# Large expert units: the 32 left-over tokens' down products in fp32 on four column strips, and two down tiles in a row

## The chip, the cores and the metric

The kernel runs on one core of one Trainium2 chip. The metric is device time in microseconds of one execution of the whole program. The trace that is read here was taken by the hardware profiler in one execution of the same kernel.

## The reference

The program is a two-layer encoder on 512 tokens of width 1024: a hybrid mixer with a dense SwiGLU, then an S5 mixer with a mixture of experts. The change is in the mixture of experts alone: 8 experts, 2 per token, inner width 3584, everything float32.

```python
def swiglu(h, w_gu, w_down):
    g, u = jnp.split(h @ w_gu, 2, axis=-1)
    return (jax.nn.silu(g) * u) @ w_down
# for each block of rows (tokens routed to expert e):  swiglu(xb, w_gu[e], w_down[e])
# out[token] += gate weight * row, over the two experts of the token
```

w_gu[e] is 1024 x 7168, w_down[e] is 3584 x 1024: 44 MB of weights per expert, which must come from HBM once for each expert.

## The kernel before

**Units.** The experts are worked one after the other as eight units, four large (i = 0, 2, 4, 6) and four small ones (i = 1, 3, 5, 7), in turn. A large unit holds CAP = 160 rows: 128 and REST = 32 left-over ones; a small unit holds 128. Rows beyond that go to extra units at the end, which the profiled run's data decide.

**Weights.** A unit's weights are PER = 42 tiles of 128 x 2048 words (1 MB). SP loads them in the order in which TensorE uses them, into a ring of RING = 6 slots (expert_tiles, L1006 to L1014). A tile's load waits until the tile six places before it is split (s_ws).

**Split.** Products run in fp32r, a form in which one product of 512 columns is one pass. To keep the accuracy of fp32, each operand is split in a high part (rounded to fp32r) and a low part (the rest). ScalarE writes the high part of a tile (split, L2545), VectorE then the low part (L3553), into WSLOTS = 3 slots. Tile n + 3 may be split once TensorE is done with tile n (s_mt). A product A x B is then three products: high x high, low x high, high x low.

**A large unit** has STEPS = 14 steps of 256 inner columns (large_pe, L1949 to L1995). Step s has a gate tile and an up tile: 32 products of 320 columns (L1984: high weights against the high and low rows) and 32 of 160 (L1986: low weights against the high rows) over banks 0 to 3. ScalarE takes the low sum out of PSUM (L2580), VectorE adds the rest to it (L3586, which counts s_gs up), ScalarE makes the Silu (L2583), VectorE the product with up (L3589, s_hid). ScalarE writes its high part (L2585), VectorE the low part (L3595, L3596; s_hdr). Each of gate and up has two halves (fb = 0, 1); before TensorE starts a gate half it waits on s_gs of the step before, since it writes over the same banks.

The tiles stand in the order gate 0, up 0, gate 1, up 1, down 0, gate 2, up 2, down 1, and so on: step s's down tile is worked behind gate and up of step s + 1. A down tile has 20 products of 512 columns in `products` (L1924), for each of 2 row blocks and 2 column halves: three for the 128 rows (banks 4, 5), and two for the left-over rows (banks 6, 7). The stationary operand of the last two is a block of 128 columns: hd[:, k, P:2P] holds the left-over rows' high part in 32 columns and their low part in the next 32, the rest is zero; hz holds the high part in 32 columns and zeros. At the end of the unit ScalarE copies the low part's products out of PSUM (L2594) and VectorE adds them to the high ones (L3605).

Between the last two down tiles TensorE transposes the rows of the next unit (turn_rows, L1932, L1936). ScalarE and VectorE bring them in high and low parts to SBUF (L2555, L3563), and the next unit's first product waits for that (rows_ready).

**A small unit** has 7 steps of 512 columns and 12 products per tile, all of them in L1924 too, and transposes of its hidden rows (L2004).

**Orders.** All engines' lists are written out by hand. In large_act and large_dve ScalarE and VectorE do, in step s: split the tile three behind the gate, the hidden rows of step s, split the tile three behind the up tile, and the one three behind the down tile. VectorE makes the low part of the hidden rows behind its split of the up tile's successor. POOL gathers the rows of the next unit (L1202, L1205) and stores the results (L1213, L1216).

**Elsewhere in the program** there is one place that already uses strips of the array: kernel_steps (L1407 to L1424) makes fp32 products with 16 stationary columns whose results go to partitions 0, 32, 64 and 96 of bank 6:

```python
        def kernel_bank(k, g, first, n):
            strip = 32 * (STEP * (k % 2) + g)
            return psum[strip:strip + GC, 6, first:first + n]
```

L1325 is a plain fp32 product of 512 columns, L1401 an fp32 transpose, L1880 the router: 4 x 8 calls of pe.matmul in fp32 with 8 stationary columns.

## Time and profile before

| what | value |
|---|---|
| median of 3 runs | 2574.84 us (2573.52 to 2577.11) |
| span of the profiled execution | 2573.5 us; the profile gives no other time of that execution |
| TensorE busy | 2442.7 us, 95% |
| VectorE, ScalarE, GpSimd busy | 65%, 50%, 8% |
| mean granted TensorE clock | 0.976 |
| HBM read, written | 496.0 MB, 45.8 MB |

The expert units run from about 1267 to 2485 us of the span. PE is TensorE, DVE VectorE, ACT ScalarE, POOL GpSimd, SPq the queue of SP. A record is one instruction as the hardware counted it; in a row, "x20" means twenty such records put together, and the duration then runs from the start of the first to the end of the last. "[0.78 <-DVE ...]" is idle time ahead of a record and what ended it.

### The profile page before, as it was taken

What the parts mean: (1) busy time and instruction counts of PE and PEld (TensorE: products, weight loads), DVE (VectorE), ACT (ScalarE), POOL (GpSimd) and SP (SyncE); (2) the same over time, 40 slices, a digit from 0 to 9 for tenths busy, and PEclk for the clock granted to TensorE, in tenths of its full rate; (3) what the DMA queues carried; (4) which work ended last, traced back from release to release, by engine and by line L of the source; (5) the groups of instructions that cost most, each with busy time, mean ns of one, the idle gap of its engine ahead of it and who ended that gap; (6) DMA issues with size and microseconds to landing.
All of it is one profiled execution on the core that took longest, in us unless ns stands there. A gap on an engine that the chain in (4) does not pass through costs nothing.

```text
span 2573.5 us, 31863 instructions
## 1 busy us (share of the span) xinstructions
PE 2442.7 (95%) x12694; PEld 1975.9 (77%) x12694; DVE 1666.8 (65%) x2031; ACT 1290.7 (50%) x1508; POOL 205.5 (8%) x204
## 2 busy tenths in 40 slices
PE   7999999999999998699699999999999999999987
PEld 4555555688888876688599888998899988998856
DVE  7996875322223343972676788668876688667865
ACT  3644351222222233662355676557765577556753
POOL 4007632000000000000100000000000000000010
PEclk9999998999999998799799999999999999999998
DMA  7669210532323224450677899778987799777961
GB/s 201 200 193 249 89 33 29 176 98 98 98 99 106 94 78 144 163 189 17 207 248 248 295 373 329 251 247 323 370 285 247 247 371 369 260 249 260 376 247 44
DMA packets 316819, 527.73 MB, mean 205 GB/s; under 512 B 19334, under 2 KB 175594, under 8 KB 314010
## 3 DMA queue, kind: packets, MB, share of 16 engines
q1 hardware_dynamic: 287594, 481.30, 54.1%
q0 software_dynamic: 5888, 25.78, 3.2%
q10 hardware_dynamic: 23184, 18.55, 2.2%
q8 instruction: 103, 1.69, 0.3%
q14 instruction: 50, 0.41, 0.0%
HBM read 496.03 MB, written 45.81 MB: 211 GB/s over the span
## 4 chain that ended last, share of the span: by engine, by line
PE 82%; DVE 10%; ACT 2%; issue 2%; POOL 2%; DMA 1%; POOLq 0%; ACTq 0%; DVEq 0%
PE psum L1924 28%; PE psum L1450 17%; PE psum L1984 12%; PE psum L1749 6%; PE psum L1986 5%; PE psum L1325 3%; PE psum L1299 2%; PE psum L2084 2%; PE psum L1522 1%; DVE stages L869 1%; DVE stages L879 1%; POOL stages L1115 1%; DVE stages L874 1%; DVE stages L870 1%; POOL stages L1118 1%
## 5 line engine op out<-in xcount | busy, mean ns | idle before, releaser
L3553 DVE TENSOR_TENSOR stages_r<-kept,stages_r 128x2048 fp32r<-128x2048 f32 x336 | 769.3, 2291 | 238.6 <-ACT stages_r L2545 237.7
L2545 ACT ACTIVATE stages_r<-kept 128x2048 fp32r<-128x2048 f32 x336 | 637.4, 1912 | 217.8 <-PE psum L1924 104.3
L1924 PE MATMUL psum<-stages_r 128*128 128x512 f32 x3136 | 738.9, 394 | 3.2 <-issue 3.2
L1924 PEld LDWEIGHTS psum<-stages_r 128*128 128x128 f32 x3136 | 584.2, 189 | 126.6 <-issue 4.7
L1984 PE MATMUL psum<-stages_r 128*128 128x320 f32 x1792 | 465.0, 345 | 4.1 <-DVE stages L3586 3.1
L1450 PE MATMUL psum<-stages_r 128*128 128x512 f32 x1920 | 437.5, 390 | 3.2 <-ACT stages_r L2111 2.7
L1986 PE MATMUL psum<-stages_r 128*128 128x160 f32 x1792 | 423.6, 236 | 0.0
L1450 PEld LDWEIGHTS psum<-stages_r 128*128 128x128 f32 x1920 | 360.1, 188 | 79.3 <-ACT stages_r L2111 3.1
L1986 PEld LDWEIGHTS psum<-stages_r 128*128 128x128 f32 x1792 | 344.0, 192 | 2.0
L3205 DVE TENSOR_TENSOR stages_r<-kept,stages_r 128x2048 fp32r<-128x2048 f32 x54 | 123.8, 2293 | 339.6 <-ACT stages_r L2403 339.6
L1984 PEld LDWEIGHTS psum<-stages_r 128*128 128x128 f32 x1792 | 337.5, 188 | 6.8 <-DVE stages_r L3553 3.8
L2403 ACT ACTIVATE stages_r<-kept 128x2048 fp32r<-128x2048 f32 x54 | 103.5, 1917 | 325.8 <-PE psum L1450 219.1
L1749 PE MATMUL psum<-stages_r,stages_front_r 128*128 128x512 f32 x672 | 152.6, 389 | 0.8 <-issue 0.8
L1749 PEld LDWEIGHTS psum<-stages_r,stages_front_r 128*128 128x128 f32 x672 | 126.1, 188 | 27.3 <-issue 1.2
L2583 ACT ACTIVATE stages<-stages 128x160 f32<-128x160 f32 x112 | 37.8, 337 | 159.6 <-DVE stages L3586 159.6
L1325 PE MATMUL psum<-stages,kept 128*128 128x512 f32 x256 | 115.5, 598 | 0.0
L1325 PEld LDWEIGHTS psum<-stages,kept 128*128 128x128 f32 x256 | 46.8, 190 | 49.6 <-issue 48.9
L1202 POOL DMA_INDIRECT stages<-moe_rows_by_token,stages x8 | 14.2, 1777 | 866.1 <-PE psum L1932 519.5
L3589 DVE TENSOR_TENSOR kept<-stages 128x160 f32<-128x160 f32 x112 | 36.7, 327 | 45.2 <-ACT stages L2583 45.2
L2097 ACT ACTIVATE stages<-kept 128x1024 f32<-128x1024 f32 x24 | 25.3, 1055 | 77.6 <-DVE kept L3199 49.1
L1522 PE MATMUL psum<-stages,kept 128*128 128x512 f32 x128 | 59.4, 594 | 0.0
L1299 PE MATMUL psum<-kept,stages 128*128 128x512 f32 x128 | 56.9, 606 | 0.8 <-DVE stages L3190 0.8
(452 smaller groups left out, 2449.9 us busy)
## 6 DMA issues: line engine op xcount, KB each, us to landing
kept<-in_moe_w_gu_dram SPq DMA_DIRECT2D x224, 1024.0 KB, 6.8
kept<-in_moe_w_down_dram SPq DMA_DIRECT2D x112, 1024.0 KB, 6.4
kept<-in_ffn_w_gu_dram SPq DMA_DIRECT2D x28, 1024.0 KB, 5.2
kept<-in_ev_w_in_dram SPq DMA_DIRECT2D x16, 1024.0 KB, 7.5
kept<-in_ffn_w_down_dram SPq DMA_DIRECT2D x14, 1024.0 KB, 5.1
s_output_maps<-s_output_maps_by_state SPq DMA_DIRECT2D x32, 256.0 KB, 4.8
kept<-s_input_maps SPq DMA_DIRECT2D x8, 1024.0 KB, 5.0
kept<-s_output_maps SPq DMA_DIRECT2D x8, 1024.0 KB, 6.0
```

The lines of the kernel that those rows point to most:

```text
L1299: m = pe.matmul(psum[:, b0 + b, 0:width], act[:, 4 * kk + k, b * P:(b + 1) * P], w[:, k, 0:width], **at)
L1325: m = pe.matmul(psum[:, b, :], *pair, start=kk == 0 and k == 0, stop=kk == 1 and k == 3)
L1450: m = pe.matmul(psum[:, 4 * (g % 2) + b, :], *pair, start=kk == 0 and k == 0 and n == 0, stop=kk == 1 and k == 3 and n == 2, skip_group_ch ...
L1522: m = pe.matmul(bank, w[:, k, b * P:(b + 1) * P], hnT[:, n, :], **at)
L1749: m = pe.matmul(psum[:, 2 * c + hf, :], a[:, k, at], w[hf][:, k, :], start=j == 0 and k == 0 and n == 0, stop=j == FJ - 1 and k == 3 and n ...
L1924: m = pe.matmul(out_, a, b, start=start and n == 0, stop=stop and n == len(pairs) - 1, skip_group_check=True)
L1984: pe.matmul(bank[:, 0:2 * CAP], wh[:, k, fs], x_[:, k, :], start=k == 0, stop=False, skip_group_check=True)
L1986: m = pe.matmul(bank[:, 0:CAP], wl[:, k, fs], x_[:, k, 0:CAP], start=False, stop=k == 7, skip_group_check=True)
L2403: act.activation(f_high[t % 2], ring[:, n % RING, :].rearrange("p (k n) -> p k n", k=4), ACT.Copy).then_inc(s_wh, 1)
L2545: act.activation(w_high[n % WSLOTS], unit_tile(n), ACT.Copy).then_inc(s_wh, 1)
L3205: dve.tensor_tensor(f_low[t % 2], ring[:, (SPLIT_RUNS[run][1] + t) % RING, :].rearrange("p (k n) -> p k n", k=4), f_high[t % 2], ALU.subtr ...
L3553: dve.tensor_tensor(w_low[n % WSLOTS], unit_tile(n), w_high[n % WSLOTS], ALU.subtract).then_inc(s_ws, 1)
```

## The change

In large units only:

- The left-over rows are no longer split. ScalarE copies them as they are to hid_rest, and the down products of these rows are made in fp32 straight from the unsplit tile in the ring: 4 products per down tile (2 row blocks x 2 column halves), each with 32 stationary columns and its own strip of 32 partitions of bank 6. The blocks of zeros and hid_z are gone, and so is POOL's writing of them.
- The order of tiles becomes gate 0, up 0, gate 1, up 1, gate 2, down 0, down 1, up 2, gate 3, up 3, gate 4, down 2, down 3, up 4, ..., gate 12, down 10, down 11, up 12, gate 13, up 13, down 12, down 13. Behind each pair of down tiles stand the fp32 products of both (rest_down), eight calls of pe.matmul.
- A down tile's slot in the ring is free only when rest_down of its pair is done: SP waits on s_rest.
- ScalarE and VectorE follow the new order tile by tile.
- The result of the left-over rows is the sum of two strips each, 64 partitions x 512, and is stored in two pieces.

```diff
-        hid_l = [hid_r[:, 1024 * n:1024 * (n + 1)].rearrange("p (f t) -> p f t", f=2) for n in range(2)]
+        hid_l = [hid_r[:, 1024 * n:1024 * n + 512].rearrange("p (f t) -> p f t", f=2) for n in range(2)]
+        hid_rest = [moa.take(2 * REST).rearrange("p (f t) -> p f t", f=2) for _ in range(2)]
...
+        large_tiles = []
+        for s_ in range(STEPS):
+            large_tiles.append(("gate", s_))
+            if s_ and s_ % 2 == 0:
+                large_tiles += [("down", s_ - 2), ("down", s_ - 1)]
+            large_tiles.append(("up", s_))
+        large_tiles += [("down", STEPS - 2), ("down", STEPS - 1)]
...
# SP, expert_tiles
                         sp.wait_ge(s_ws, i * PER + (SPLIT0 + n + 1 - RING))
+                        owner, before = (i, n - RING) if n >= RING else (i - 1, PER + n - RING)
+                        if large(owner) and large_tiles[before][0] == "down":
+                            sp.wait_ge(s_rest, RESTS * (owner // 2) + rest_behind(large_tiles[before][1]))
...
# POOL
-            for pads in (hid_r, hz_r):
-                blocks = pads.rearrange("p (n t) -> p n t", t=P)
-                zero = ident.unsqueeze(1).broadcast_to([P, blocks.shape[1], P])
-                m = pool.tensor_tensor(blocks, zero, zero, ALU.subtract)
-            m.then_inc(s_rz, 1)
...
-                    pool.dma_start(y_rows[b:b + REST, :], yblk[0:REST, 1, :]).then_inc(s_mys, 16)
+                    for hf in range(2):
+                        pool.dma_start(y_rows[b:b + REST, 512 * hf:512 * (hf + 1)],
+                                       yblk[REST * hf:REST * (hf + 1), 1, 0:512]).then_inc(s_mys, 16)
...
# TensorE, down(s_)
-                            products(psum[:, 4 + hf, :], ((hd[:, k, 0:P], wh[:, k, at]), (hd[:, k, 2 * P:3 * P], wh[:, k, at]),
-                                                          (hd[:, k, 0:P], wl[:, k, at])), first, last_)
-                            m = products(psum[:, 6 + hf, :], ((hd[:, k, P:2 * P], wh[:, k, at]), (hz[:, k, :], wl[:, k, at])),
-                                         first, last_)
+                            m = products(psum[:, 4 + hf, :], ((hd[:, k, 0:P], wh[:, k, at]), (hd[:, k, P:2 * P], wh[:, k, at]),
+                                                              (hd[:, k, 0:P], wl[:, k, at])),
+                                         s_ == 0 and k == 0, s_ == STEPS - 1 and k == 1)
+                    m.then_inc(s_mt, 1)
+
+                def rest_down(*steps):
+                    for s_ in steps:
+                        w = unit_tile(large_at["down", s_]).rearrange("p (k n) -> p k n", k=2)
+                        for k in range(2):
+                            for hf in range(2):
+                                strip = REST * (2 * k + hf)
+                                m = pe.matmul(psum[strip:strip + REST, 6, :], hid_rest[s_ % 2][:, k, :], w[:, k, 512 * hf:512 * (hf + 1)],
+                                              start=s_ == 0, stop=s_ == STEPS - 1, skip_group_check=True)
+                    m.then_inc(s_rest, 1)
...
+                for s_ in range(STEPS):
+                    gate_up(0, s_)
+                    if s_ and s_ % 2 == 0:
+                        down(s_ - 2)
+                        down(s_ - 1)
+                        rest_down(s_ - 2, s_ - 1)
+                    gate_up(1, s_)
+                down(STEPS - 2)
                 pe.wait_ge(s_gs, 2 * STEPS * (li + 1))
                 turn_rows(i + 1)
                 down(STEPS - 1)
+                rest_down(STEPS - 2, STEPS - 1)
...
# ScalarE, large_act
-                    act.activation(hid_l[s_ % 2][:, :, 0:CAP], lhid, ACT.Copy)
-                    act.activation(hid_z[s_ % 2][:, :, 0:REST], lhid[:, :, P:CAP], ACT.Copy).then_inc(s_hdA, 1)
+                    act.activation(hid_l[s_ % 2][:, :, 0:P], lhid[:, :, 0:P], ACT.Copy)
+                    act.activation(hid_rest[s_ % 2], lhid[:, :, P:CAP], ACT.Copy).then_inc(s_hdA, 1)
+
+                for n, (what, s_) in enumerate(large_tiles):
+                    if what == "up":
+                        hidden(s_, n)
+                    if n == PER - 1:
+                        rows_high(i + 1)
+                    split(i, n + WSLOTS)
                 used(i, PER - 1)
                 y_rows_free(i)
-                act.activation(low_rows[0:REST, :], psum[REST:2 * REST, 6:8, :].rearrange("p b n -> p (b n)"),
-                               ACT.Copy).then_inc(s_ysh, 1)
                 act.activation(yblk[:, 0, :], psum[:, 4:6, :].rearrange("p b n -> p (b n)"), ACT.Copy).then_inc(s_myA, 1)
+                act.wait_ge(s_rest, RESTS * (li + 1))
+                act.activation(low_rows, psum[2 * REST:P, 6, :], ACT.Copy).then_inc(s_ysh, 1)
...
# VectorE, large_dve
+                for n, (what, s_) in enumerate(large_tiles):
+                    last = s_ == STEPS - 1
+                    if what == "up":
+                        hidden(s_)
+                        if last:
+                            hidden_low(s_)
+                    if n == PER - 1:
+                        rows_low(i + 1)
+                    split(i, n + WSLOTS)
+                    if what == "up" and not last:
+                        hidden_low(s_)
```

## Rows read from the trace of the kernel before

**Rows 1.** Page, sections 1 and 4: busy time by engine; chain by line.
```profile
PE 2442.7 (95%) x12694; PEld 1975.9 (77%) x12694; DVE 1666.8 (65%) x2031; ACT 1290.7 (50%) x1508; POOL 205.5 (8%) x204
PE psum L1924 28%; PE psum L1450 17%; PE psum L1984 12%; PE psum L1749 6%; PE psum L1986 5%; PE psum L1325 3%; PE psum L1299 2%; PE psum L2084 2%; PE psum L1522 1%; DVE stages L869 1%; DVE stages L879 1%; POOL stages L1115 1%; DVE stages L874 1%; DVE stages L870 1%; POOL stages L1118 1%
```

**Rows 2.** Stretches of a large and a small unit: us, busy by engine, PEclk, DMA share, GB/s.
```profile
1575.20:1750.60 175.40, 174.62 (x1157) 163.79 (x1156) 121.26 (x126) 104.27 (x126) 0.58 (x1) 1.00 0.75 257
1750.60:1877.70 127.10, 126.31 (x577) 103.86 (x576) 110.60 (x64) 94.05 (x65) 6.35 (x5) 1.00 0.99 358
```

**Rows 3.** Timeline of PE, two down tiles: start us, us, what, count [idle before].
```profile
1605.36 4.78 PE L1924 MATMUL psum<-stages_r 128*128 128x512 f32 x20
...
1618.15 4.78 PE L1924 MATMUL psum<-stages_r 128*128 128x512 f32 x20
```

**Rows 4.** Timeline of PE, gate tile 1 behind up tile 0.
```profile
1583.31 0.23 PE L1986 MATMUL psum<-stages_r 128*128 128x160 f32 x1
1584.32 0.38 PE L1984 MATMUL psum<-stages_r 128*128 128x320 f32 x1 [0.78 <-DVE stages L3586]
```

**Rows 5.** Line 1880, the router: count, ns min/median/max, first and last start.
```profile
L1880 PE MATMUL psum<-stages x64: 269/273/275, 1232.3 to 1240.3; 128*8 128x128 f32 x64
```

**Rows 6.** Timeline of PE, plain fp32 products of 512 columns.
```profile
125.52 4.45 PE L1325 MATMUL psum<-kept,stages 128*128 128x512 f32 x10
```

**Rows 7.** Timeline of PE around strips: transposes, strips, small products.
```profile
95.48 1.04 PE L1401 MATMUL psum<-kept,stages 128*128 128x128 f32 x8
96.45 0.63 PE L1414 MATMUL psum<-stages 128*16 128x128 f32 x16
97.01 0.23 PE L1422 MATMUL psum<-kept,stages 16*16 16x16 f32 x8
```

**Rows 8.** Line 1414: its weight loads.
```profile
L1414 PEld LDWEIGHTS psum<-stages x176: 91/97/98, 70.1 to 197.1; 128*16 128x16 f32 x176
```

**Rows 9.** Timeline of ACT, hidden rows of one step.
```profile
1606.44 0.42 ACT L2580 ACTIVATE stages<-psum 128x320 f32<-128x320 f32 x1
1608.15 0.47 ACT L2585 ACTIVATE stages_r<-kept 128x320 fp32r<-128x320 f32 x1 [0.39 <-DVE kept L3589]
1608.68 3.70 ACT L2545 ACTIVATE stages_r<-kept 128x2048 fp32r<-128x2048 f32 x2
```

**Rows 10.** Timeline of DVE, around the stall, of one step, and at a unit's end.
```profile
1583.69 0.48 DVE L3586 TENSOR_TENSOR stages<-psum,stages 128x320 f32<-128x320 f32 x1
...
1606.89 0.49 DVE L3586 TENSOR_TENSOR stages<-psum,stages 128x320 f32<-128x320 f32 x1
1607.79 0.33 DVE L3589 TENSOR_TENSOR kept<-stages 128x160 f32<-128x160 f32 x1 [0.40 <-ACT stages L2583]
1610.61 2.29 DVE L3553 TENSOR_TENSOR stages_r<-kept,stages_r 128x2048 fp32r<-128x2048 f32 x1 [2.49 <-ACT stages_r L2545]
1612.82 0.42 DVE L3595 TENSOR_TENSOR stages_r<-kept,stages_r 128x256 fp32r<-128x256 f32 x1
...
1755.66 1.28 DVE L3563 TENSOR_TENSOR stages_r<-psum,stages_r 128x512 fp32r<-128x512 f32 x2
```

**Rows 11.** Timeline of PE, the end of a large unit and six tiles of the next.
```profile
1750.63 1.04 PE L1932 MATMUL psum<-kept,stages 128*128 128x128 f32 x8
1751.43 4.82 PE L1924 MATMUL psum<-stages_r 128*128 128x512 f32 x20
1757.04 16.91 PE L1924 MATMUL psum<-stages_r 128*128 128x512 f32 x72 [0.79 <-issue]
...
1774.14 0.48 PE L1924 MATMUL psum<-stages_r 128*128 128x512 f32 x1
```

**Rows 12.** Loads of the expert units: issue of one, and time from issue to landing of all.
```profile
1743.60 0.37 SPq L1014 DMA_DIRECT2D kept<-in_moe_w_gu_dram  x1
...
DMA to landing us min/median/max: 4.9/6.6/13.9
```

**Rows 13.** DMA queues, 1756 to 1878 us: packets, MB, share of 16 engines.
```profile
q1 hardware_dynamic: 20246, 43.27, 97.8%
```

More of the change, by code:

```diff
@@ L289, in build_program @@
         s_gu = sem("first_chunk_gate_up_done")
+        s_rest = sem("leftover_down_rows_done")
         s_tb = sem("low_token_part_copied")
@@ L549, in build_program @@
         ptok1 = moa.take(1024).rearrange(v4, a=4)
-        hz_r = both(2 * 256)[1]
-        hid_z = [hz_r[:, 256 * n:256 * (n + 1)].rearrange("p (f t) -> p f t", f=2) for n in range(2)]
+        hid_rest = [moa.take(2 * REST).rearrange("p (f t) -> p f t", f=2) for _ in range(2)]
         work = moa.take(2048)
@@ L600, in build_program, with rest_behind @@
         moe_dram = nc.dram_tensor("moe_rows_by_token", (T, D), F32, kind="Internal").ap()
-        def gate_at(s_):
-            return max(3 * s_ - 1, 0)
-        def down_at(s_):
-            return min(3 * s_ + 4, PER - 1)
+        large_tiles = []
[5 more added lines that the diff above has]
+        large_tiles += [("down", STEPS - 2), ("down", STEPS - 1)]
+        RESTS = STEPS // 2
+        def rest_behind(s_):
+            return s_ // 2 + 1
+        large_at = {tile: n for n, tile in enumerate(large_tiles)}
+        assert len(large_tiles) == PER
         def sgate_at(s_, kk):
@@ L641, in dn @@
                 return w_edn[bass.ds(e, 1), EF * s_:EF * (s_ + 1), :].rearrange("a (k p) n -> p (a k) n", p=P)
-            tiles = []
-            for s_ in range(STEPS):
-                tiles += [up(EF * s_), up(EF * (STEPS + s_))]
-                if s_:
-                    tiles.append(dn(s_ - 1))
-            return tiles + [dn(STEPS - 1)]
+            return [dict(gate=lambda: up(EF * s_), up=lambda: up(EF * (STEPS + s_)), down=lambda: dn(s_))[what]()
+                    for what, s_ in large_tiles]
         def small_sources(e):
@@ L667, in build_program @@
         GATHERS = [sum(1 + large(n) for n in range(i + 1)) for i in range(NE)]
+        STORES = [sum(1 + 2 * large(n) for n in range(i + 1)) for i in range(NE)]
         def gathers_done(i):
@@ L1954, in down @@
                 def down(s_):
-                    n = down_at(s_)
+                    n = large_at["down", s_]
                     pe.wait_ge(s_ws, i * PER + (SPLIT0 + n + 1))
@@ L1960, in down @@
                     wh, wl = weights(n, 2)
-                    hd, hz = hid_l[s_ % 2], hid_z[s_ % 2]
+                    hd = hid_l[s_ % 2]
                     for k in range(2):
@@ new lines, in gate_up @@
+                def gate_up(part, s_):
+                    n = large_at[("gate", "up")[part], s_]
+                    pe.wait_ge(s_ws, i * PER + (SPLIT0 + n + 1))
+                    wh, wl = weights(n, 8)
+                    for fb in range(2):
+                        if part == 0 and s_:
+                            pe.wait_ge(s_gs, 2 * (STEPS * li + s_ - 1) + fb + 1)
+                        fs = slice(P * fb, P * (fb + 1))
+                        bank = psum[:, 2 * part + fb, :]
+                        for k in range(8):
+                            pe.matmul(bank[:, 0:2 * CAP], wh[:, k, fs], x_[:, k, :], start=k == 0, stop=False,
+                                      skip_group_check=True)
+                            m = pe.matmul(bank[:, 0:CAP], wl[:, k, fs], x_[:, k, 0:CAP], start=False, stop=k == 7,
+                                          skip_group_check=True)
+                        if part == 1 and fb == 0:
+                            m.then_inc(s_gu, 1)
@@ L2563, in y_rows_free, with hidden @@
                 if not isinstance(i, int):
-                    act.wait_ge(s_mys, i * 16 + (FILLED + 16 * (GATHERS[NE - 1] - NE)))
+                    act.wait_ge(s_mys, i * 16 + (FILLED + 16 * (STORES[NE - 1] - NE)))
                 elif i:
-                    act.wait_ge(s_mys, FILLED + 16 * GATHERS[i - 1])
+                    act.wait_ge(s_mys, FILLED + 16 * STORES[i - 1])
             def large_act(i):
                 li = i // 2
-                for s_ in range(STEPS):
-                    n = gate_at(s_)
-                    split(i, n + WSLOTS)
+                def hidden(s_, n):
                     for fb in range(2):
@@ L2576, in large_act @@
                         if fb:
-                            used(i, n + 1)
+                            used(i, n)
                         else:
@@ L3572, in y_rows_free, with hidden @@
                 if not isinstance(i, int):
-                    dve.wait_ge(s_mys, i * 16 + (FILLED + 16 * (GATHERS[NE - 1] - NE)))
+                    dve.wait_ge(s_mys, i * 16 + (FILLED + 16 * (STORES[NE - 1] - NE)))
                 elif i:
-                    dve.wait_ge(s_mys, FILLED + 16 * GATHERS[i - 1])
+                    dve.wait_ge(s_mys, FILLED + 16 * STORES[i - 1])
             def large_dve(i):
                 li = i // 2
-                for s_ in range(STEPS):
-                    n = gate_at(s_)
-                    split(i, n + WSLOTS)
+                def hidden(s_):
                     for fb in range(2):
```

44 lines of the change are left out of this document (5 added, 39 removed).

## The prediction

> **What bounds the kernel now.** I read the page first. TensorE is busy for 95% of the span, and L1924, the line of all products of down tiles and of the small units, has 28% of the chain that ended last [rows 1]. Busy time alone doesn't say whether less work on TensorE is less time, so the next view is the table of stretches. A large unit (1575.20 to 1750.60) has TensorE busy for 174.6 of 175.4 us, VectorE for 121.3 and the DMA engines at 0.75; the small unit behind it has TensorE at 126.3 of 127.1 and the DMA engines at 0.99 [rows 2]. TensorE sets the pace of both; in large units the others have room on average, in small ones the DMA has none. The timeline gives the beat. The 20 products of a down tile start at 1605.36 and take 4.78 to the end of the last, which is 0.39; so they follow each other by (4.78 - 0.39) / 19 = 0.231, 4.62 for the tile. The next down tile starts at 1618.15 [rows 3], 12.79 later, which leaves 8.17 for gate and up together, 4.09 each. A step is 12.79 us and nothing is waited for in it.
>
> One place shows what comes if a gate tile follows an up tile with no down tile between, as in each large unit's first two steps: TensorE stands from 1583.31 to 1584.32, released by the sum that VectorE makes of gate and up (L3586) [rows 4]. It is there once per large unit. The change puts every gate tile but the first in that place.
>
> **Products.** Removed: 8 of 20 products in each of 14 down tiles of 4 units, 448 x 0.231 = 103.4 us. Added: 4 fp32 products of 32 columns per down tile, in 28 groups of two tiles. The trace shows each part. An fp32 product is two records: the router's 32 calls stand as 64 [rows 5]. A 512-column record starts (4.45 - 0.59) / 9 = 0.429 after the one before [rows 6], so one call costs 0.86 alone. L1414 is already this form: fp32, 128 rows, 16 columns, four column strips of bank 6. Its 16 records of 128 columns take 0.63 from first start to last end, of which the last is 0.27 [rows 7, 8]. One after the other they would start 0.11 apart, as L1401's do ((1.04 - 0.27) / 7), over 1.65; they start over 0.36, which is three steps of 0.11 and a skew, four at a time. A new group has 16 records as well: 4 x 0.429 = 1.72. Changing the array's form costs on either side: L1401's last start is 96.25, L1414's first 96.45, 0.20 for 0.11, and L1414's last (96.81) to L1422's first (97.01) is again 0.20 [rows 7]. With 0.09 twice and 0.02 of skew a group costs 1.93, and 28 cost 54.0. Bounds: 1.72 a group, 48 us, if both changes hide; one record at a time, 16 x 0.429 = 6.86, 192 us. I take 1.93, since L1414 differs only in length and in 16 for 32 columns.
>
> TensorE's work thus falls by 103.4 - 54.0 = 49.4 us. This is what the change would give if nothing waited.
>
> **The wait at every second gate tile.** Take an even step s, with down tiles between its gate and its up, and call the end of its up tile 0. Gate s+1 runs to 4.09, up s+1 to 8.17, and gate s+2 must wait for L3586's first sum of step s+1 [rows 4]. VectorE's list before that sum is now longer. With the rows of one step [rows 9, 10]: ScalarE copies the second low sum from 0.20 to 0.64 (L2580), VectorE adds to 1.16 (0.49 behind 0.03), the Silu lies in the 0.41 until the product starts, which ends at 1.90 (0.33). The hidden copies today take 0.53 from 1608.15 to the split's start at 1608.68; the first gets a fifth shorter (256 elements for 320, 0.07 less), so the split starts at 1.93 + 0.46 = 2.39. ScalarE's split of gate s+2 (1.91) ends at 4.30, VectorE's (2.29) at 6.62, the low part of hidden s (L3595, 0.42) at 6.96, then VectorE's split of the next down tile, which ScalarE has had ready since 6.3, at 9.17, and the sum at 9.58. TensorE starts 0.14 later (1583.69 + 0.48 to 1584.32 [rows 4, 10]), at 9.72. That is 1.55 after 8.17, and 0.09 more goes into refilling (the first gate and up behind today's stall take 8.26, not 8.17): 1.64. At the first such gate, where step 0 has no group ahead of it, the same list gives about 1.48. At gates of odd steps nothing waits: with two down tiles and a group (7.5 us) before the up tile, VectorE's splits are done by the middle of it. Per unit: 1.48 + 5 x 1.64 = 9.7; over four units 38.7. Bounds: below, today's stall of 1.0 at each, 24.7 us; above, 2.29 more if one more split gets ahead of the sum, 94 us. The value is from the list, since its every length is a row.
>
> **Two down tiles in a row.** The second of a pair needs the hidden rows of the step just before. From the sum's end they need 7.2 us by the same list (2.0 until the hidden product, 0.5 until the split, then 1.92, 2.29 and 0.42); gate and first down tile give 4.09 + 0.09 + 2.77, so 0.1 is waited, 6 times per unit. At the unit's end a down tile of 2.77 for 4.62 and the transposes (0.79) [rows 11] no longer cover it: 0.9, with 0.1 for refilling. Over four units 6.6 us; bounds 0 and 4 x (6 x 1 + 2) = 32. Then the next unit: its first product waits until VectorE has split two tiles and written the low rows (L3563, 1.28 [rows 10]). Counted from the end of the last up tile that is 11.7, where TensorE is done at 9.3 with the group: 2.3 waited. Today 20 products from 1751.43 end at 1756.05 and the next start at 1757.04 [rows 11], 1.0. So 1.35 more, 5.4 over four units; bounds 0 and 12.
>
> **The ring.** A down tile's slot was free once it was split; now it is free when its group is done. SP's new wait on s_rest stands ahead of every later load, since SP has one list. Within a unit it costs nothing: the blocked load lands 5 to 7 us after the group [rows 12], and its split may start 8.2 after it. At the unit's end the small unit's tile 4 was asked for at 1743.60, 13.4 us ahead of its first product; now it is 2.0 ahead. It lands some 3.3 to 5 us behind that first product, split and ready at 8 to 9.5; it is needed at 4 x 2.8 = 11.1. I cost it at nothing (TensorE's four tiles hide it) and price its loss below. Behind ScalarE's new wait on s_rest stand its copy of the rows and then the split of tile 3, which must wait for TensorE's tile 0 anyway. The second store on POOL's queue (0.6 us of issue per large unit) and the zeroing that POOL loses are work of an engine that is busy for 8% [rows 1]: 0, bounds -1 and +1.
>
> **Sum.** -103.4 + 54.0 + 38.7 + 6.6 + 5.4 = +1.3. The profiled span of 2573.5 becomes 2574.8; the runs' median is 1.3 above that span, so 2576.1. The forecast: no change, because what TensorE saves is stood out again at every second gate tile. A pair of steps shows it: 25.57 us now, 16.34 + 5.54 + 1.93 + 1.64 + 0.1 = 25.55 then.
>
> **Where the skill differs.** "TensorE: Matmul & The Clock Gate" of the Trainium skill, Part 3 (The mechanism; Measured speedup vs the span model), says that a weight load overlaps running products only if it goes to other row groups, which strips of columns share, and gives 2.38 times for three column strips of 512. At that efficiency a group would be an estimated 2.2 + 0.2, the sum some 13 us more. Rows 7 and 8 speak against it: with weight loads of 0.097, L1414's foursomes still follow 0.11 apart.
>
> **Rivals.**
> - Faster: the stall stays what the one row shows, 1.03 with refilling, because the other splits and the low part find their places before the up tile. Then 24 x 0.6 = 14.6 less than forecast, 2562. For it: it is the only measured case. Against: there VectorE had only ScalarE's lateness to wait for (the split before it was 2.29 and the sum 0.48 [rows 10]); the list above has 2.3 + 0.4 more in front.
> - Slower, weight loads: each foursome waits for its own load, 4 x 0.097 = 0.39 a group, x 28 = 10.9, 2587. This is the page's rule as a mechanism. Against it stand the rows just named; for it, that 32 columns and 512-column streams are in no row.
> - Slower, the ring: small units start with slots 4 and up empty. They read 43.3 MB in 122 us with the queue at 97.8% [rows 13], 2.9 us a tile of 1.05 MB at most, beside TensorE's 2.85 (17.1 from 1757.04 to the end of the transposes at 1774.14 for six tiles [rows 11]). The margin is 2 to 3 us over 38 tiles. It decides once the DMA's pace is above 2.85 + 2.6/38 = 2.92; at 3.0 it costs 38 x 0.15 - 2.6 = 3.1 a unit, 12 in all: 2588.
> - Much slower: the strips don't overlap at 512 columns, 28 x (6.86 - 1.74) = 143 more, 2719. Only that L1414 is short speaks for it.
>
> **How the numbers follow.** About 0.2%, 5 us, is what a measurement of this kernel can tell from no change. Forecast 0.50, its own range 2569 to 2582 (a tenth of a microsecond in the stall is 2.4 us, in a group 2.8); of it 0.42 lies within the 5 us, 0.05 below and 0.03 above. Faster rival 0.20, weight loads 0.12, ring 0.13, no overlap 0.03, something unseen and slower 0.02. Faster 0.25, same 0.42, slower 0.33. The range leaves out the no-overlap case and some of each side: 2562 to 2589.
>
> **What would show it.** Right: pairs of steps at 25.5 to 25.7 us on TensorE; 16 fp32 records of a group over 1.7 to 1.8 us; a stall of 1.4 to 1.7 before each even gate released by L3586's successor, none before odd gates; large units near 174, small ones near 128, with ScalarE never released by a DMA. Wrong: pairs under 25; records of a group more than 0.45 apart; any split that waits for a landing in a small unit; a second stall of half a microsecond or more in a pair.

## The result, and the profile after

The kernel after takes 2582.6 us (median of 8 runs, 2580.2 to 2586.0), the kernel before, measured beside it, 2577.3 (median of 8, 2573.5 to 2580.0). The ratio is 1.0022, with an interval of 1.0012 to 1.0033: slower by 5.3 us. The forecast was 2576.1, with 2569 to 2582 as its own range and 2562 to 2589 with most of the rivals. So the sign of the small sum came out as forecast (+1.3) and its size is 4 us short. The change is just over the 0.2% that I had set as the bound of no change, and its interval (3 to 8 us) reaches to both sides of that bound. The profiled execution took 2582.35 us, its span 2580.7. Two kernels further down had one execution each that took far longer than its other three (5291 and 3987 us); their medians are of the other three.

Busy time by engine and the chain by engine, from the page of the kernel after:

```profile
PE 2409.2 (93%) x12694; PEld 1901.4 (74%) x12694; DVE 1658.2 (64%) x1975; ACT 1293.8 (50%) x1508; POOL 196.8 (8%) x206
PE 69%; DVE 19%; ACT 6%; issue 3%; POOL 2%; DMA 1%; ACTq 0%; POOLq 0%; DVEq 0%
```

TensorE is busy for 33.5 us less than before [rows 1], and the span is 7.2 us longer. The work went and the time didn't. The two stretches that answer to [rows 2]:

```profile
1578.60:1752.80 174.20, 165.59 (x1149) 146.25 (x1149) 119.14 (x110) 103.70 (x123) 0.59 (x1) 1.00 0.73 249
1752.80:1882.20 129.40, 126.51 (x585) 102.74 (x585) 110.71 (x66) 95.32 (x68) 4.62 (x6) 1.00 1.00 366
```

In the large unit TensorE now stands for 8.6 us where it stood for 0.8. The small unit is no longer full either: 2.9 us idle. One step pair on TensorE, answering to [rows 3, 4] (start us, us, what, count [idle before]):

```profile
1621.49 0.23 PE L1999 MATMUL psum<-stages_r 128*128 128x160 f32 x1
1623.06 0.38 PE L1997 MATMUL psum<-stages_r 128*128 128x320 f32 x1 [1.33 <-DVE stages L3607]
...
1627.20 5.87 PE L1930 MATMUL psum<-stages_r 128*128 128x512 f32 x24
1633.00 1.92 PE L1983 MATMUL psum<-kept,stages 128*32 128x512 f32 x16
1634.86 0.42 PE L1997 MATMUL psum<-stages_r 128*128 128x320 f32 x1
```

Three things are to be seen. The gap in front of an even gate tile is 1.57 from the last start of the up tile (1621.49) to the first of the gate (1623.06), where [rows 4] had 1.01; 0.07 of either is the usual distance between two such products. The two down tiles are 24 products over 5.80. The group's first record starts at 1633.00 and the next up tile's first product at 1634.86, 1.86 later, so the 16 fp32 records do run four at a time. And this is VectorE's list in front of that gate, answering to [rows 10], with ScalarE's copy of the low sum that the last entry adds to:

```profile
1614.02 0.49 DVE L3607 TENSOR_TENSOR stages<-psum,stages 128x320 f32<-128x320 f32 x1 [0.83 <-ACT stages L2601]
...
1617.68 2.29 DVE L3575 TENSOR_TENSOR stages_r<-kept,stages_r 128x2048 fp32r<-128x2048 f32 x1 [2.44 <-ACT stages_r L2567]
1619.89 0.42 DVE L3616 TENSOR_TENSOR stages_r<-kept,stages_r 128x256 fp32r<-128x256 f32 x1
1620.23 2.28 DVE L3575 TENSOR_TENSOR stages_r<-kept,stages_r 128x2048 fp32r<-128x2048 f32 x1
1622.43 0.48 DVE L3607 TENSOR_TENSOR stages<-psum,stages 128x320 f32<-128x320 f32 x1
...
1619.71 0.44 ACT L2601 ACTIVATE stages<-psum 128x320 f32<-128x320 f32 x1
```

It is the list of the prediction, entry for entry: the split of the gate tile, the low part of the hidden rows, the split of the next down tile, and only then the sum that TensorE waits for. The sum starts 0.94 after the last product of the up tile started, because VectorE is at the split in front of it (2.28 from 1620.23) until then, not because its own data are late: ScalarE's low sum is ready at 1620.15. The handover to the small unit, answering to [rows 11]:

```profile
1754.54 2.96 PE L1930 MATMUL psum<-stages_r 128*128 128x512 f32 x12 [0.69 <-DVE stages_r L3616]
1757.44 1.92 PE L1983 MATMUL psum<-kept,stages 128*32 128x512 f32 x16
...
1761.57 0.93 PE L1930 MATMUL psum<-stages_r 128*128 128x512 f32 x3 [2.21 <-issue]
```

### The profile page after: what moved, and what is told of

The parts are those of the page before. It is cut to its first block, busy times and chain, and to the rows that moved or that the text cites. A ratio compares the mean times of both kernels' runs of the same rounds, so it can differ in the third digit from the quotient of the medians.

```text
span 2580.7 us, 31865 instructions
## 1 busy us (share of the span) xinstructions
PE 2409.2 (93%) x12694; PEld 1901.4 (74%) x12694; DVE 1658.2 (64%) x1975; ACT 1293.8 (50%) x1508; POOL 196.8 (8%) x206
## 4 chain that ended last, share of the span: by engine, by line
PE 69%; DVE 19%; ACT 6%; issue 3%; POOL 2%; DMA 1%; ACTq 0%; POOLq 0%; DVEq 0%
PE psum L1930 24%; PE psum L1456 17%; PE psum L1997 6%; PE psum L1755 5%; DVE stages_r L3575 5%; PE psum L1999 2%; ACT stages_r L2567 2%; PE psum L1305 2%; PE psum L1983 2%; PE psum L2106 1%; PE psum L1331 1%; PE psum L1528 1%; DVE stages L3607 1%; DVE stages L875 1%; DVE stages L885 1%
## 5 line engine op out<-in xcount | busy, mean ns | idle before, releaser
L2567 ACT ACTIVATE stages_r<-kept 128x2048 fp32r<-128x2048 f32 x336 | 642.8, 1914 | 182.9 <-PE psum L1930 152.6
L1930 PE MATMUL psum<-stages_r 128*128 128x512 f32 x2688 | 637.0, 395 | 11.6 <-issue 8.8
L1930 PEld LDWEIGHTS psum<-stages_r 128*128 128x128 f32 x2688 | 500.7, 189 | 127.8 <-issue 23.0
L1997 PE MATMUL psum<-stages_r 128*128 128x320 f32 x1792 | 470.2, 348 | 35.4 <-DVE stages L3607 34.5
L1456 PE MATMUL psum<-stages_r 128*128 128x512 f32 x1920 | 437.5, 390 | 3.2 <-ACT stages_r L2133 2.7
L1456 PEld LDWEIGHTS psum<-stages_r 128*128 128x128 f32 x1920 | 359.9, 188 | 79.5 <-ACT stages_r L2133 3.1
L1997 PEld LDWEIGHTS psum<-stages_r 128*128 128x128 f32 x1792 | 337.2, 188 | 60.2 <-DVE stages_r L3575 59.0
L1999 PEld LDWEIGHTS psum<-stages_r 128*128 128x128 f32 x1792 | 343.0, 191 | 0.1
L1331 PE MATMUL psum<-stages,kept 128*128 128x512 f32 x256 | 115.5, 598 | 0.0
L2601 ACT ACTIVATE stages<-psum 128x320 f32<-128x320 f32 x112 | 48.4, 432 | 70.5 <-PE psum L1999 68.1
L3607 DVE TENSOR_TENSOR stages<-psum,stages 128x320 f32<-128x320 f32 x112 | 54.7, 488 | 26.2 <-ACT stages L2601 26.2
```

What stands on the lines that cost most here:

```text
L1331: m = pe.matmul(psum[:, b, :], *pair, start=kk == 0 and k == 0, stop=kk == 1 and k == 3)
L1456: m = pe.matmul(psum[:, 4 * (g % 2) + b, :], *pair, start=kk == 0 and k == 0 and n == 0, stop=kk == 1 and k == 3 and n == 2, skip_group_ch ...
L1930: m = pe.matmul(out_, a, b, start=start and n == 0, stop=stop and n == len(pairs) - 1, skip_group_check=True)
L1997: pe.matmul(bank[:, 0:2 * CAP], wh[:, k, fs], x_[:, k, :], start=k == 0, stop=False, skip_group_check=True)
L1999: m = pe.matmul(bank[:, 0:CAP], wl[:, k, fs], x_[:, k, 0:CAP], start=False, stop=k == 7, skip_group_check=True)
L2567: act.activation(w_high[n % WSLOTS], unit_tile(n), ACT.Copy).then_inc(s_wh, 1)
```

## The experiments

Kernels that were measured together share the runs of the kernel before; its medians were 2579.2 us (beside order_only, strips_by_step, sum_first and one_strip), 2579.3 (beside rows_first, by_step_rows_first, sums_first_all and no_ring_hold) and 2578.9 (beside the last three). The ratios are to these. Edits are to the kernel after unless said otherwise. "Pair" is two steps of a large unit.

### The order alone, without the strips

The eight old products of the left-over tokens stay; only the order of the tiles is new.

```
-                    hd = hid_l[s_ % 2]
+                    hd, hz = hid_l[s_ % 2], hid_z[s_ % 2]
...
+                            m = products(psum[:, 6 + hf, :], ((hd[:, k, P:2 * P], wh[:, k, at]), (hz[:, k, :], wl[:, k, at])),
+                                         first, last_)
...
-                        rest_down(s_ - 2, s_ - 1)
...
-                rest_down(STEPS - 2, STEPS - 1)
```

> The new order of tiles alone; the left-over rows go back to 8 split products per down tile. Theory (the list of VectorE): every gate tile that stands right behind an up tile waits for VectorE's sum. Before even gates 1.5 us; before odd gates too, about 1.0, because without the fp32 group the up tile starts right behind the second down tile and VectorE's splits reach into it. 6 x 1.6 + 6 x 1.0 per large unit with refilling, less what is hidden elsewhere: 14 to 15 us a unit, 57 to 61 in all, 2636 or so. Rival, that only the even gates wait (the sum as it was forecast for the changed kernel): 24 x 1.6 = 39, 2616. Rival, that the order costs nothing and the fp32 products are what is slow: within 5 us of the kernel before.

2642.3 us, 1.0243 [1.0226, 1.0260]: 63 us slower than before. Line L1989, the gate and up products of 320 columns, from the table by line (busy, mean ns | idle just before them), and one gate tile of an odd step from the timeline:

```profile
L1989 PE MATMUL psum<-stages_r 128*128 128x320 f32 x1792 | 470.1, 347 | 57.1 <-DVE stages L3598 56.2 <-ACT stages_r L2571 1.0
```
```profile
1659.35 0.23 PE L1991 MATMUL psum<-stages_r 128*128 128x160 f32 x1
1660.41 0.38 PE L1989 MATMUL psum<-stages_r 128*128 128x320 f32 x1 [0.82 <-DVE stages L3598]
```

The order costs 57.1 - 4.1 = 53 us of plain standing, nearly all of it released by the sum. Here odd gates wait too (1.06 from start to start). The strips take that wait away: their group gives TensorE 1.85 us of work between the second down tile and the up tile, and VectorE's last split ahead of the sum starts 0.26 us behind the up tile's start (1609.42 and 1609.16) where it starts 2.2 behind it here (1657.57 and 1655.36). That is read off the two traces; no run tests it alone. So the kernel after is two halves of opposite sign: an order that loses 63 us, and strips that win some 57 in it (the ratios 1.0243 and 1.0022, apart by 0.0221 x 2577).

### The strips alone, in the old order

```
-            large_tiles.append(("gate", s_))
-            if s_ and s_ % 2 == 0:
-                large_tiles += [("down", s_ - 2), ("down", s_ - 1)]
-            large_tiles.append(("up", s_))
+            large_tiles += [("gate", s_), ("up", s_)]
+            if s_:
+                large_tiles.append(("down", s_ - 1))
...
+                    if s_:
+                        down(s_ - 1)
+                        rest_down(s_ - 1)
```

> The fp32 products on strips alone, in the order of tiles of before: each down tile behind its up tile, its own four products right behind it. Theory: the products are worth what was worked out (103.4 us removed; 56 groups of 8 records at 0.86 + 0.19 = 1.04, 58 us, added), no gate but gate 1 waits, the handover to the small unit costs 1.4 more, 4 times: 2577 - 103 + 58 + 6 = 2538; with the clock falling in one handover and some refilling up to 2545. Rival, that strips cost more than their records tell, or that the ring's later release binds: 2555 or more.

2551.2 us, 0.9890 [0.9873, 0.9907]: 28 us faster than before. That is 6 us above the upper end of what I had expected (2538 to 2545), and on the near side of the rival's 2555. One step on TensorE:

```profile
1585.91 2.96 PE L1929 MATMUL psum<-stages_r 128*128 128x512 f32 x12
1588.80 1.06 PE L1982 MATMUL psum<-kept,stages 128*32 128x512 f32 x8
1589.79 0.41 PE L1996 MATMUL psum<-stages_r 128*128 128x320 f32 x1
1598.08 2.96 PE L1929 MATMUL psum<-stages_r 128*128 128x512 f32 x12
```

Nothing stands in it, so it measures the strips bare. The down tile takes 2.89 to the group, where 12 x 0.231 is 2.77. The group takes 0.99. Gate and up take 8.29 (1589.79 to 1598.08), where the kernel before has 8.17. A group therefore costs 0.12 ahead of it and 0.12 behind it over its own records, whether it has 8 or 16: this is the term that I had too small, 56 x 0.19 = 11 us in this kernel (1.00 + 0.23 where I had 1.04). The other shortfall is in the handover, and the granted clock shows it (us, busy by engine, PEclk, DMA share, GB/s):

```profile
1739.65 1.06 PE L1982 MATMUL psum<-kept,stages 128*32 128x512 f32 x8
1742.97 18.45 PE L1929 MATMUL psum<-stages_r 128*128 128x512 f32 x72 [2.26 <-issue]
```
```profile
1742.90:1746.40 3.50, 3.43 (x9) 2.76 (x10) 2.76 (x2) 0.37 (x1) 0.16 (x1) 0.56 0.94 310
2039.90:2043.30 3.40, 3.40 (x10) 2.71 (x9) 2.37 (x2) 0.00 (x0) 0.45 (x1) 0.55 1.04 367
2336.80:2340.30 3.50, 3.50 (x11) 2.74 (x10) 2.11 (x2) 0.00 (x0) 0.79 (x2) 0.56 1.07 409
```

Behind three of its four handovers the clock falls from 2.4 to 1.2 GHz for some 3.4 us. The 72 products of the first three tiles take 18.45 instead of 16.91 [rows 11], 1.5 us each time.

### The order of the change, with the sum ahead of the split

In odd steps but the last VectorE makes the two sums and the two products with up before it splits the down tile that isn't needed yet.

```
                 for n, (what, s_) in enumerate(large_tiles):
                     last = s_ == STEPS - 1
+                    if what == "gate" and s_ % 2 and not last:
+                        continue
                     if what == "up":
                         hidden(s_)
                         if last:
                             hidden_low(s_)
+                        elif s_ % 2:
+                            split(i, n - 1 + WSLOTS)
```

> The changed kernel with one thing moved in VectorE's list: in odd steps but the last its split of the next down tile stands behind the sums and the hidden product instead of ahead of them. Theory: the even gates' stalls of 1.5 us (24 of them) go, but for 0.2 us before the first down tile, whose split is now late: about 36 to 38 us less than the changed kernel, 2545. Rival, that the stall only moves to the down tiles because VectorE is short of time as a whole: 2575 or more.

2552.1 us, 0.9897 [0.9881, 0.9914]: 30 us off the kernel after by moving one VectorE instruction behind four others.

```profile
L1997 PE MATMUL psum<-stages_r 128*128 128x320 f32 x1792 | 467.0, 347 | 4.1 <-DVE stages L3607 3.1 <-ACT stages_r L2581 1.0
```

The idle time in front of gate products is back to the 4.1 us of the kernel before, from 35.4: the stall belongs to VectorE's list and not to the new order itself. This is the run that names the cause. The later split costs little: it ends just ahead of the first down tile, which loses about 0.1 us by it (I had allowed 0.2).

```profile
1635.98 2.28 DVE L3575 TENSOR_TENSOR stages_r<-kept,stages_r 128x2048 fp32r<-128x2048 f32 x1
```
```profile
1638.32 5.94 PE L1930 MATMUL psum<-stages_r 128*128 128x512 f32 x24
```

My 2545 is missed by 7 us. In the traces a pair is 1.42 shorter and a large unit, to the small unit's first product, 8.3 (182.9 to 174.6), 33 us over four where I had expected 36 to 38; the kernel before was 2 us slower here than beside the kernel after. The form changes and the long handovers are in both kernels and don't explain it; the rest, some 2 us, stays open.

### One strip for four

```
-                                strip = REST * (2 * k + hf)
+                                strip = 0
```

> The changed kernel with all fp32 products of the left-over rows on the first strip (the other strips' results are left out, so these rows come out wrong). If the four strips work at once in the changed kernel, a group of 16 records now takes 16 x 0.429 = 6.9 us for 1.85: 28 x 5.0 = 140 more, 2722. Rival, that records of one strip overlap too and the strips are not what makes it fast: no change, 2583.

2722.9 us (one run), within 1 us of the expected. One group:

```profile
1642.26 7.05 PE L1983 MATMUL psum<-kept,stages 128*32 128x512 f32 x16
```

7.05 against 1.92, each from the first start to the last end: on one strip the same 16 records follow each other. The rival without overlap was priced rightly (2719), and it isn't what happens with four strips.

### The next unit's rows one tile earlier

In both engines' lists the copies of the next unit's rows go ahead of the last but one split. Once with the sum ahead of the split, once in the old order of tiles:

```
-                    if n == PER - 1:
+                    if n == PER - 2:
                         rows_high(i + 1)      (ScalarE)
...
-                    if n == PER - 1:
+                    if n == PER - 2:
                         rows_low(i + 1)       (VectorE)
```

> sum_first and one move more: ScalarE and VectorE bring the next unit's rows to SBUF ahead of their split of the next unit's second tile, not behind it. Theory: the small unit's first product waits 2.3 us for the low rows, and in some units the idle time lets the granted clock fall to 1.2 GHz for 3.4 us, another 1.6. The move takes about 2.2 us per unit from the wait and with it the clock's fall: 9 to 12 us less than sum_first, 2541. Rival, that something else (the fp32 group, the landing of tile 4) holds the small unit: no change from sum_first.

> strips_by_step with the same move of the next unit's rows. Its handovers stand 2.3 us each and in its profile the clock fell in three of four (1.57 us each). Expected: 4 x 2.0 and up to 4 x 1.6 less, 11 to 13, 2539. The rival as above: no change.

2541.4 us, 0.9857 [0.9837, 0.9877], and 2540.0 us, 0.9850 [0.9830, 0.9870], three executions each. Both gain some 11 us over their parents. Three handovers of the first, by stretch:

```profile
1736.00:1746.00 10.00, 10.00 (x52) 6.81 (x51) 9.53 (x7) 8.56 (x9) 1.60 (x3) 1.00 0.71 238
2032.00:2042.00 10.00, 10.00 (x52) 7.07 (x53) 9.00 (x7) 8.56 (x7) 1.62 (x3) 1.00 0.77 271
2325.00:2335.00 10.00, 10.00 (x52) 6.93 (x51) 9.30 (x7) 8.56 (x7) 1.55 (x3) 1.00 0.66 234
```

The wait of 2.3 us is gone, and with it the falls of the clock. The two orders come out at the same time, as far as these runs can tell. So the order of the change has neither merit nor cost of its own once VectorE's list suits it: a pair takes 24.3 us in both. Down tiles in twos halve the changes of form, and lose most of that again to the late split and to the hidden rows (5.87 for 24 products, where 5.54 and 0.12 were due).

Something else comes in with this move. In the first of the two ScalarE's splits now wait for landings (us in total, times, longest; most of it costs TensorE nothing), where sum_first had 2.8 us of it and the kernel after none:

```profile
ACT stages_r L2567 <- DMA kept<-in_moe_w_gu_dram: 33.3, 33, 3.0
```

### The sums ahead in step 0 too, with and without SP's wait

The first kernel gives step 0 what odd steps have; this takes away the stall that the kernel before has as well [rows 4]. Two more remove SP's wait on s_rest, once from the kernel after and once from this one.

```
-                    if what == "gate" and s_ % 2 and not last:
+                    if what == "gate" and (s_ % 2 or not s_) and not last:
...
-                        elif s_ % 2:
+                        elif s_ % 2 or not s_:
```
```
-                        owner, before = ...
-                        if large(owner) and large_tiles[before][0] == "down":
-                            sp.wait_ge(s_rest, ...)
...
-                        w = unit_tile(large_at["down", s_]).rearrange("p (k n) -> p k n", k=2)
+                        w = pw1
```

> rows_first, and VectorE's split is put behind the sums in step 0 as well, so that the old stall of 1.0 at gate 1 of each large unit goes: 3 to 4 us less than rows_first, 2537. Rival, that up 1 then waits for its late split by as much: no change from rows_first.

> The changed kernel, but the fp32 products of the left-over rows read a fixed 128 x 2048 tile of SBUF (other weights, so these rows come out wrong) and SP doesn't wait on s_rest: a slot is free once split, as before the change. If the ring's later release costs nothing, as was forecast: within 2 us of the changed kernel, some 5 us above the kernel before. Rival, that the late loads at the handover or the bursts inside large units cost: 5 us or more less than the changed kernel.

> sums_first_all, its fp32 products reading a fixed tile of SBUF (those rows come out wrong) and SP not waiting on s_rest. If the late loads of the small units come from the ring's later release, ScalarE is no longer released by landings and the time falls by 4 to 6 us, 2535; in the changed kernel itself the same edit changed nothing. Rival, that the DMA is too slow for small units whatever the ring does: no change from sums_first_all, 2540.

> sums_first_all once more, beside the other two on the same chip, since the difference looked for is 5 us: 2540, with ScalarE released by landings in the first tiles of each small unit.

Removing the wait from the kernel after changes nothing: 2583.2 us, 1.0020 [1.0009, 1.0032]. SP's wait costs it nothing, as forecast. The sums ahead in step 0 bring 2540.5 and, repeated, 2540.3 us (0.9857 [0.9840, 0.9873] and 0.9850 [0.9837, 0.9863]), 1 us where 3 to 4 were expected. In the traces the stall at gate 1 is gone and each large unit is 0.8 us shorter, 3.1 in all; the small units give 0.3 of it back. So the gain is there, and the run medians are too coarse to show it. What ScalarE's splits wait for hasn't changed from the kernel with the rows earlier; in the repeated run:

```profile
ACT stages_r L2567 <- DMA kept<-in_moe_w_gu_dram: 33.9, 33, 3.2
```

and how one such wait reaches TensorE, in the first run (ScalarE, VectorE, TensorE):

```profile
1758.98 1.92 ACT L2567 ACTIVATE stages_r<-kept 128x2048 fp32r<-128x2048 f32 x1 [1.22 <-DMA kept<-in_moe_w_down_dram]
```
```profile
1760.93 2.29 DVE L3575 TENSOR_TENSOR stages_r<-kept,stages_r 128x2048 fp32r<-128x2048 f32 x1 [1.21 <-ACT stages_r L2567]
```
```profile
1763.37 6.88 PE L1930 MATMUL psum<-stages_r 128*128 128x512 f32 x29 [1.12 <-DVE stages_r L3575]
```

The ring is now a limit at the start of a small unit: slots come free only with the last group, and a load lands just too late. Without SP's wait the same kernel takes 2539.2 us (0.9850 [0.9836, 0.9863]), 1 us less, where I had expected 4 to 6. The two intervals lie on each other, so the run times can't tell nothing from 3 us. The traces can: without the wait no landing releases ScalarE in the expert units, and the small units take 2.9 us less over all four. One of them, from its first product to the next unit's first gate product, with the wait and without:

```profile
1740.30:1862.10 121.80, 121.21 (x553) 99.23 (x550) 106.51 (x61) 89.15 (x61) 2.62 (x4) 1.00 1.04 382
```
```profile
1738.00:1858.70 120.70, 120.70 (x551) 99.39 (x550) 106.46 (x61) 89.25 (x61) 2.61 (x4) 1.00 1.02 368
```

So the ring's later release costs about 3 us here, in one profiled execution of each.

### The last group cut in two

The version the experiments point to: the kernel with the sums ahead in step 0, and the fp32 products of down tile 12 right behind it, ahead of the transposes; those of tile 13 last. SP counts one group more per unit.

```
+                rest_down(STEPS - 2)
...
-                rest_down(STEPS - 2, STEPS - 1)
+                rest_down(STEPS - 1)
```

> sums_first_all, with the last group of a large unit in two: the fp32 products of step 12 stand right behind its down tile, ahead of the transposes, so that the small unit's tile 4 is asked for some 6 us earlier; they also lie in the 0.95 us for which TensorE waits for the last hidden rows. Theory: in sums_first_all ScalarE waits 8 us for landings in the small unit and TensorE stands 1.1 to 1.5 us once per small unit; that goes, 4 to 6 us less than sums_first_all, 2535. Rival, that one tile earlier doesn't help a queue that is full anyway: same as sums_first_all.

2537.0 us (2536.1 to 2539.5), 0.9841 [0.9827, 0.9854]: the lowest median of the study, 42 us under the kernel before and some 46 under the kernel after. It is 3.3 us under its parent, where 4 to 6 were expected, and the intervals of the two overlap. The ring slot of down tile 12 comes free earlier, and eight of the strips' records cover the wait for the last hidden rows:

```profile
1728.69 2.93 PE L1930 MATMUL psum<-stages_r 128*128 128x512 f32 x12
1731.56 1.06 PE L1983 MATMUL psum<-kept,stages 128*32 128x512 f32 x8
1732.55 1.09 PE L1938 MATMUL psum<-kept,stages 128*128 128x128 f32 x8
1733.40 3.00 PE L1930 MATMUL psum<-stages_r 128*128 128x512 f32 x12
1736.33 1.06 PE L1983 MATMUL psum<-kept,stages 128*32 128x512 f32 x8
1738.01 16.88 PE L1930 MATMUL psum<-stages_r 128*128 128x512 f32 x72 [0.61 <-issue]
```
```profile
ACT stages_r L2568 <- DMA kept<-in_moe_w_gu_dram: 5.8, 5, 1.6
```
```profile
1566.40:1731.50 165.10, 165.10 (x1149) 146.09 (x1147) 119.17 (x110) 104.53 (x123) 0.59 (x1) 1.00 0.77 261
1731.50:1858.60 127.10, 126.49 (x585) 102.66 (x585) 110.69 (x66) 95.27 (x68) 5.86 (x6) 1.00 1.02 373
```

ScalarE waits for landings for 5.8 us instead of 33.9, and the small units take what they took without SP's wait. In a large unit TensorE stands for nothing. One large and one small unit take 292.2 us together (165.1 + 127.1), 10.3 fewer than in [rows 2] (302.5). In the small unit TensorE stands for 0.6 us and the DMA engines are full, so neither has room there.

## Why the prediction was right or wrong

**Removed work.** Right. 448 products are gone at 0.231 each; the down tiles of a pair take 5.80 for 24 products. TensorE's busy time fell by 33.5 us only, and not by 49.4, since busy time also holds what the waits and the changes of form stretch: as an estimate from the terms below, 4 for the form changes, 4 for the parts of the 24 stalls that lie under the record ahead, 2 for refilling, 3 for the down tiles and 1.5 for the clock, together some 15 of the 16 us.

**A group on the strips: the mis-sized term.** I took 1.72 for the records, 0.02 of skew and 0.09 for each change of the array's form, 1.93 in all. The records came nearly as said (1.85 for 16 up to the next product's start; I had named 1.7 to 1.8). The changes cost more, by the bare step of the strips alone: 0.12 lie in the down tile ahead and 0.12 in the gate and up tiles behind, beside the 0.13 that 1.85 holds over 1.72. A group costs 1.85 + 0.23 = 2.08. That is 0.15 more than I had, x 28 = 4.2 us. That it equals the whole miss of 4 us is partly luck: the account below has two more terms, of opposite sign. The step that failed, a matter of size and not of mechanism, was reading the price of a form change off products of 128 columns [rows 7]: they have weights and columns of another length on both sides, and no row of before shows 512 columns next to strips.

**The stall at even gates.** Right. Forecast, with refilling, 1.48 at gate 2 and 1.64 at gates 4 to 12; measured 1.41 and 1.59 (from start to start 1.44 and 1.57, less the usual 0.07, and the rest of the 18.04 us of two gates and two ups over 4 x 4.09 and the form change). None at odd gates. The faster rival (1.03, as in [rows 4]) falls: VectorE's three entries in front of the sum are all there. With the split moved behind the sums, 31 us of idle time went (35.4 to 4.1) and 30 us of the time.

**The second down tile and the unit's end.** Near enough: a pair's down tiles have 0.13 more than the form change explains (forecast 0.1), and from the first transpose to the last down tile it is 1.72 for 0.80, 0.92 more (1.0 with refilling).

**A pair.** 18.04 for two gates and two ups with the stall, 5.79 and 1.85, 25.69 in all. That is inside the 25.5 to 25.7 I named and 0.14 above the 25.55 of the sum.

**The handover.** The size was right, 4.13 from the group's first record to the small unit's first product (1757.44 to 1761.57), 2.3 of it waited. What I had not seen is its follow-up. After one of the four, in the profiled execution, the clock fell:

```profile
1452.30 1.92 PE L1983 MATMUL psum<-kept,stages 128*32 128x512 f32 x16
1456.43 18.46 PE L1930 MATMUL psum<-stages_r 128*128 128x512 f32 x72 [2.21 <-issue]
```
```profile
1456.40:1459.80 3.40, 3.37 (x8) 2.73 (x9) 2.73 (x2) 0.31 (x1) 0.08 (x1) 0.51 1.03 395
1761.50:1764.90 3.40, 3.33 (x15) 2.77 (x16) 2.76 (x2) 0.34 (x1) 0.06 (x1) 1.00 1.02 387
```

8 products in 3.4 us instead of 15, and 18.46 for 72 instead of 16.91: 1.5 us. The other three handovers of that execution have the same stand and kept 2.4 GHz.

**The ring.** Right for the kernel after: no landing releases ScalarE in a unit, and without SP's wait the time is the same. The ring rival had its place right and its condition wrong. I had it decide once the DMA's pace rose above 2.92 us a tile; it decided once TensorE had nothing else to stand for. In sum_first, with large units 8.3 us shorter, ScalarE waits 2.8 us for landings; with the stand of the handover gone too it waits 33, in all three kernels that keep SP's wait with the last group whole and the pairs of down tiles.

**The weight loads.** The strips' loads are hidden:

```profile
L1983 PEld LDWEIGHTS psum<-kept,stages x448: 106/110/110, 1302.1 to 2365.5; 128*32 128x32 f32 x150
```

110 ns each, while 16 records take 1.85 us, 0.13 over 4 x 0.429, so the products of the four strips overlap and no foursome waits for its loads. "TensorE: Matmul & The Clock Gate" of the Trainium skill, Part 3 (Measured speedup vs the span model), gives 2.38 times for three strips of columns; here four give 7.05 / 1.92 = 3.7 times, and the measurement decides. The extra 0.15 a group is a cost of the change of form, not of loads: it is the same with 8 records as with 16.

**The account.** From the first gate product of one large unit to that of the next (behind the last, to TensorE's first product after its small unit), before: 304.5, 302.5, 302.5, 305.1 us; after: 307.2, 303.6, 303.6, 306.3. The four together are 6.0 longer, forecast 1.3. Of the 4.7 between, 4.2 are the form changes, 1.5 the clock in the first unit, and about 1 goes back because the stalls were 0.05 shorter, x 24. The span has another 1.2 us ahead of the first unit and behind the last; that is outside the change and I have no cause for it.

## What to carry to other kernels

When an order of tiles is changed, write out the in-order list of every engine that feeds the waiting one, and ask of each entry whether anybody needs it yet: here one 2.29 us split ahead of a 0.49 us sum took back 30 us of what the strips had won. Where a change of two parts moves nothing, run each part alone before judging either: alone the parts were worth +63 and -28 us. They don't add up to the +5 of both, because the strips also take waits away that the order brings. Once the large wait was gone, small ones (the next unit's rows, gate 1, the last hidden rows and the ring behind them) were worth another 15 us.

## What the runs showed that I had not expected

- The clock fell from 2.4 to 1.2 GHz behind a stand of TensorE of only 2.2 to 2.3 us, for some 3.4 us, at a price of 1.5 us. In the profiled executions it did so behind one of four handovers of the kernel after, of the same without SP's wait and of sum_first, and behind three of four with the strips in the old order: 6 of 16 with that stand. It did so behind none with a stand of 1.4 us (order_only), 0.8 (before) or 0.6 and less. Of handovers with the same stand, some fell and some didn't; no run settles why.
- A change between the whole array and four column strips costs TensorE 0.23 us over the group's own time in a row of 512-column and 320-column products, and part of it shows as slower neighbours, 0.12 in the tile ahead and 0.12 in the tiles behind, not as a gap.
- Four fp32 column strips of 32 columns run as one stream: 16 records take 1.92 us on four strips, 7.05 on one.
